# The first head of a two-layer attention trunk: other loading order, two tiles projected together

## The reference, cut to what matters

```python
D_MODEL, SEQ, DEPTH, N_HEADS, HEAD_DIM = 1024, 512, 2, 8, 128
for i in range(DEPTH):                      # layer 0: MoBA attention, layer 1: forgetting attention
    hdn = rms_norm(x, norm_g[i])
    proj = hdn @ w_in[i]                    # 1024 x 4096 (layer 1: 8 columns more)
    q, k, v, z = split(proj, 4)             # 8 heads of 128 columns each
    q = rms_norm(split_heads(q), q_norm)    # layer 0: then rotary, by cos and sin tables
    k = rms_norm(split_heads(k), k_norm)
    y = attention(q, k, v)                  # 512 positions, causal
    y = merge_heads(y) * silu(z)
    x = x + y @ w_out[i]
```

## Time and profile before

| | |
|---|---|
| median of the runs | 595.29 us |
| the profiled execution | 596.05 us |
| its span on the core | 594.3 us |
| PE busy | 579.3 us, 97% of the span |
| DVE, POOL, ACT busy | 343.6, 267.3, 249.1 us |

### The profile page before, as it was taken

One profiled execution on the slowest core, in us unless ns is written; L12 is line 12 of the kernel. 1 busy time (PEld: TensorE's weight loads), 2 busy tenths in 40 slices (PEclk: granted clock), 3 DMA queues, 4 the chain that ended last, 5 costly groups with the idle time before them and its releaser, 6 DMA issues.

```text
span 594.3 us, 9968 instructions
## 1 busy us (share of the span) xinstructions
PE 579.3 (97%) x3219; PEld 538.6 (91%) x3219; DVE 343.6 (58%) x825; ACT 249.1 (42%) x759; POOL 267.3 (45%) x318
## 2 busy tenths in 40 slices
PE   5799999999999999999999999999999999999998
PEld 4689999999999999888899799999999999998887
DVE  4946766767685949464640074747473737373721
ACT  5535353536262635242541254445362626351500
POOL 4664554536372827063662053536362627270600
PEclk9899999999999999999996699999999999999999
DMA  9532322223131313024422024422331335131221
GB/s 284 152 106 81 99 66 77 72 71 88 53 88 53 104 38 124 18 72 137 120 70 75 0 72 71 75 69 60 83 88 53 88 53 90 51 107 34 72 89 53
DMA packets 77195, 48.36 MB, mean 81 GB/s; under 512 B 4080, under 2 KB 71408, under 8 KB 77168
## 3 DMA queue, kind: packets, MB, share of 16 engines
q1 hardware_dynamic: 77168, 48.02, 30.1%
HBM read 45.91 MB, written 2.10 MB: 81 GB/s over the span
## 4 chain that ended last, share of the span: by engine, by line
PE 88%; DVE 4%; DMA 3%; SPq 2%; ACT 1%; issue 1%; POOL 1%
PE banks L295 24%; PE banks L297 24%; PE banks L296 24%; PE banks L402 5%; PE banks L387 3%; PE banks L354 2%; DMA w_raw<-in_b_w_in_dram 2%; PE banks L372 2%; PE banks L376 2%; PE banks L371 2%; DMA first_raw<-in_a_w_in_dram 1%; SPq L230 1%; DVE probs L677 1%; PE banks L375 1%; DVE hT_lo L685 1%
## 5 line engine op out<-in xcount | busy, mean ns | idle before, releaser
L959 POOL TENSOR_TENSOR w_lo<-w_raw,w_hi 128x512 fp32r<-128x512 f32 x152 | 193.6, 1302 | 69.3 <-ACT w_hi L524 69.3
L295 PE MATMUL banks<-w_hi,hT_hi 128*128 128x384 f32 x512 | 176.5, 345 | 6.9 <-DVE qkn L740 5.3
L296 PE MATMUL banks<-w_lo,hT_hi 128*128 128x384 f32 x512 | 172.3, 337 | 0.0
L297 PE MATMUL banks<-w_hi,hT_lo 128*128 128x384 f32 x512 | 172.3, 336 | 0.0
L974 POOL TENSOR_TENSOR msq<-ssq,eps 128x2 f32<-128x2 f32 x64 | 13.9, 217 | 206.6 <-ACT junk L551 206.6
L295 PEld LDWEIGHTS banks<-w_hi,hT_hi 128*128 128x128 f32 x512 | 97.2, 190 | 8.1 <-DVE qkn L740 6.0
L524 ACT ACTIVATE w_hi<-w_raw 128x512 fp32r<-128x512 f32 x152 | 87.4, 646 | 24.1 <-DMA w_raw<-in_b_w_in_dram 14.4
L296 PEld LDWEIGHTS banks<-w_lo,hT_hi 128*128 128x128 f32 x512 | 97.0, 190 | 0.0
L297 PEld LDWEIGHTS banks<-w_hi,hT_lo 128*128 128x128 f32 x512 | 96.8, 189 | 0.0
L551 ACT ACTIVATE junk<-banks 128x128 bf16<-128x128 f32 x128 | 34.3, 274 | 121.4 <-PE banks L297 121.4
L818 DVE RECIPROCAL gz<-gz 128x128 f32<-128x128 f32 x64 | 58.1, 930 | 0.5
(11 more groups left out here) (107 smaller groups left out, 931.7 us busy)
## 6 DMA issues: line engine op xcount, KB each, us to landing
w_raw<-in_b_w_in_dram SPq DMA_DIRECT2D x64, 256.0 KB, 3.7
w_raw<-in_a_w_in_dram SPq DMA_DIRECT2D x56, 256.0 KB, 3.0
w_raw<-in_w_out_dram SPq DMA_DIRECT2D x32, 256.0 KB, 2.9
xs<-in_x_dram SPq DMA_DIRECT2D x4, 512.0 KB, 6.6
first_raw<-in_a_w_in_dram SPq DMA_DIRECT2D x8, 256.0 KB, 5.8
out_dram<-xs SPq DMA_DIRECT2D x7, 256.0 KB, 2.1
gz<-in_norm_g_dram SPq DMA_DIRECT2D x2, 512.0 KB, 4.4
cos_t<-in_rope_cos_dram SPq DMA_DIRECT2D x1, 256.0 KB, 5.5
```

Of the source, the lines that this page charges most:

```text
L295: pe.matmul(dst, ah, bh, start=first and m == 0, stop=False)
L296: pe.matmul(dst, ah, bl, start=False, stop=False)
L297: mm = pe.matmul(dst, al, bh, start=False, stop=last and m == n - 1)
L959: pool.tensor_tensor(w_lo[:, slot, k, :], raw, f32(w_hi[:, slot, k, :]), ALU.subtract).then_inc(wlo_set, by)
```

## The change

It touches only the first head of layer 0; everything from `turn_qk` of head 0 on is issued as before.

- SP: x0 and x1 are loaded ahead of w0 to w7, then x2, tables, x3, and the weights of head 1, whose last four chunks go into `first_raw` (`load_second`). The 512 KB transfer that spread the norm weight goes; ACT issues one row of 4 KB instead.
- PE: two matmuls of 512 columns against a row of ones spread the norm weight into PSUM banks 2 and 5 (`spread_gain`); 2 warm-up transposes instead of 19; tiles 0 and 1 are turned first and projected together, chunk by chunk; each tile of head 0 has its own bank (0, 1, 2, 5), so `qkv` waits for no `qkn_set` there. `zproj` of head 0 writes bank 2 and waits for `qkn_set` 3.
- DVE: both first tiles are normalised before the splits; `norm_x` reads the norm weight from PSUM; chunks 3, 5, 7 of the weights are split on DVE, for head 1 too.
- POOL: chunks 0, 1, 2, 4, 6; the sin tables (four operations) as well as the cos tables, after the factor of tile 3.

```diff
-WARM_UPS = 19
+WARM_UPS = 2
+POOL_FIRST = {0: 1, 1: 1, 2: 2, 4: 2, 6: 2}
+DVE_FIRST = (3, 5, 7)
...
+        def qkv_bank(layer, h, t):
+            return (0, 1, 2, 5)[t] if layer == 0 and isinstance(h, int) and h == 0 else t % 2
...
+            def load_second():
+                for k in range(RAW):
+                    load_chunk(w_raw[:, k, :], head_src(0, 1)(k), raw_in[k])
+                sp.wait_ge(wlo_set, 4)
+                sp.wait_ge(wlo_odd, 1)
+                for k in range(RAW, KC):
+                    load_chunk(first_raw[:, k - RAW, :], head_src(0, 1)(k), first_in[k - RAW])
...
             load_x(0)
-            sp.dma_start(gz[:, :, :].rearrange("p a n -> p (a n)"),
-                         norm_g[0].partition_broadcast(P)).then_inc(gain_in[0], 16)
-            load_first(range(0, 4))
             load_x(1)
-            load_first(range(4, 6))
+            load_first(range(KC))
             load_x(2)
-            load_first(range(6, KC))
             load_tables()
             load_x(3)
+            load_second()
             load_forget()
-            load_job(0, 1, head_src(0, 1))
+            sp.wait_ge(wlo_odd, 2 * len(DVE_FIRST))
...
+            def spread_gain():
+                pe.wait_ge(gain_in[0], 16)
+                for half in range(2):
+                    mm = pe.matmul(banks[:, GAIN_BANKS[half], :], f32(pick[0:1, 0, :]), gz[0:1, half, :],
+                                   start=True, stop=True)
+                mm.then_inc(gain_spread, 1)
...
                 wait(pe, gate_set, g)
+                if isinstance(g, int) and g == 0:
+                    pe.wait_ge(qkn_set, 3)
...
+                    spread_gain()
                     warm_up()
                     turn_hidden(layer, 0)
-                    for t in range(TILES):
-                        qkv(layer, 0, 0, t, (lambda: turn_hidden(layer, t + 1)) if t + 1 < TILES else None)
+                    turn_hidden(layer, 1)
...
+                    for k in range(2, KC):
+                        first_w(0, k)
+                        qkv_part(layer, 0, 0, 0, (k,))
+                        qkv_part(layer, 0, 0, 1, (k,))
+                        if k == 6:
+                            turn_hidden(layer, 2)
+                    pe.wait_ge(xn_set, 2 * TILES)
+                    qkv_part(layer, 0, 0, 2, range(4))
+                    turn_hidden(layer, 3)
+                    qkv_part(layer, 0, 0, 2, range(4, KC))
+                    qkv_part(layer, 0, 0, 3, range(KC))
...
# ACT, first(0):
                     square_x(layer, 0)
-                    split_w(layer, 0, 0, (0, 1))
+                    square_x(layer, 1)
+                    split_w(layer, 0, 0, (0,))
                     split_hidden(layer, 0)
...
+                    split_w(layer, 0, 0, (2, 3, 4, 5))
                     square_x(layer, 2)
+                    split_w(layer, 0, 0, (6, 7))
+                    square_x(layer, 3)
+                    split_hidden(layer, 2)
+                    read_qkv(layer, 0, 0, 0)
+                    read_qkv(layer, 0, 0, 1)
+                    split_w(layer, 1, 1, (0, 1))
+                    split_hidden(layer, 3)
...
# DVE, first(0):
                     norm_x(layer, 0)
-                    split_w_odd((1,))
+                    norm_x(layer, 1)
                     split_hidden(layer, 0)
...
+                    split_first_w(0, (3, 5))
                     norm_x(layer, 2)
+                    split_first_w(0, (7,))
+                    scale_gain()
+                    norm_x(layer, 3)
                     split_hidden(layer, 2)
...
```

More of the change, by code:

```diff
@@ L317, in turn_hidden, with qkv_part @@
                     mm.then_inc(hT_turned, 1)
[L319 to L328, removed]
+            def qkv_part(layer, h, slot, t, ks):
+                for k in ks:
@@ L335, in qkv @@
                                  (w_hi[:, slot, k, 0:3 * P], w_lo[:, slot, k, 0:3 * P]))], k == 0, k == KC - 1)
-                mm.then_inc(a_done, 1)
+                if k == KC - 1:
+                    mm.then_inc(a_done, 1)
+            def qkv(layer, h, slot, t):
+                a = TILES * (HEADS * layer + h) + t
+                wait(pe, qkn_set, a - 1)
+                if isinstance(a, int) and a == TILES:
+                    for k in range(KC):
+                        first_w(1, k)
+                        qkv_part(layer, h, slot, t, (k,))
+                    return
+                if t == 0:
+                    pe.wait_ge(wlo_set, KC * (JOBS * layer + h + 1))
+                qkv_part(layer, h, slot, t, range(KC))
@@ L338, in zproj, with first_w @@
+            def first_w(j, k):
+                if k in DVE_FIRST:
+                    pe.wait_ge(wlo_odd, len(DVE_FIRST) * j + DVE_FIRST.index(k) + 1)
+                else:
+                    pe.wait_ge(wlo_set, KC * j + sum(by for n, by in POOL_FIRST.items() if n <= k))
             def zproj(layer, h, slot):
@@ L670, in norm_x @@
                 buf = normed(layer, t)
+                if layer == 0:
+                    dve.wait_ge(gain_spread, 1)
+                    gain = [banks[:, b, :] for b in GAIN_BANKS]
+                else:
+                    dve.wait_ge(gain_in[layer], 16)
+                    gain = [gz[:, half, :] for half in range(2)]
                 dve.wait_ge(xrs_set, n + 1)
-                dve.wait_ge(gain_in[layer], 16)
                 wait(dve, hT_turned, 2 * (n - 1) if layer or t == 3 else 0)
@@ L722, in norm_qk @@
                     for m in range(2):
-                        last = dve.scalar_tensor_tensor(out=qkn[:, t, m, :], in0=banks[:, t % 2, m * P:(m + 1) * P],
+                        last = dve.scalar_tensor_tensor(out=qkn[:, t, m, :], in0=banks[:, qkv_bank(layer, h, t), m * P:(m + 1) * P],
                                                         scalar=rstd[:, t % 2, m:m + 1], in1=cos_t[:, 0, m, :],
@@ L999, in first @@
                     rstd_x(layer, 0)
[L1000 removed]
                     rstd_x(layer, 1)
[L1002 to L1003 removed]
+                    for k, by in POOL_FIRST.items():
+                        if k == 6:
+                            rstd_x(layer, 2)
+                        split_w(layer, 0, 0, (k,), by=by)
+                    rstd_x(layer, 3)
                     pool.wait_ge(tables_set, 1)
+                    half = P // 2
                     for m in range(2):
+                        for a in range(2):
+                            pool.tensor_tensor(sin_t[:, :, m, a * half:(a + 1) * half],
+                                               sin_t[:, :, 1, a * half:(a + 1) * half],
+                                               bcast(gains[:, m, (1 - a) * half:(2 - a) * half], TILES), ALU.mult)
                         folded = pool.tensor_tensor(cos_t[:, :, m, :], cos_t[:, :, 1, :],
```

136 lines of the change are left out of this document (68 added, 68 removed).

## The result

The changed kernel took 588.87 us (median of 4 runs, 587.64 to 588.92), the kernel before, beside it on the same chip, 595.19 (595.04 to 595.59). The ratio is 0.9883, 95% interval 0.9871 to 0.9895: faster by 6.3 us, where 8.8 were forecast. The time lies inside the range of 584.6 to 590.4, but outside the likeliest case's own range of 585.4 to 587.6, by 1.3 us.

What follows compares the result with a forecast made beforehand. PE bounds the kernel, with 15.0 us idle, nearly all in the first head. `turn_qk` moving from 46.66 to 37.9 saves 8.8 us: 595.29 - 8.8 = 586.5 us, range 584.6 to 590.4.

Steps and rivals of the forecast that it cites:

- the likeliest case: Head 0: z begins between 31.3 and 33.5 us, total 585.4 to 587.6 us; chance 0.55.
- Each microsecond earlier there is one off the total: PE reaching `turn_qk` of head 0 earlier shortens the total equally; 46.66 to 37.9 us gives 8.8 us.
- signs of being wrong: New profile: clock 0.5 beyond 16 us, tile 2 after 23, new PE waits after `turn_qk`, sin above 1.2, x3 after 19.
- signs of being right: `turn_qk` near 37.9, 0.8 us `qkn` wait before z, none before tiles, sin 0.8 near 19.8, normalisation at 7.3, halves 0.74.
- Rival 4: PE in head 0: without 17 warm-ups the clock never rises, `turn_qk` at 57.5, 606.1 us; chance 0.03 with other losses.
- The spread and the normalisations: PE and DVE, head 0: norm weight spread by two matmuls, ready at 7.3 us; each normalisation half takes 0.74 us.
- The pair: PE projects tiles 0 and 1 together from 11.7 us, until 20.9, or 22.3 with the first three microseconds at low clock.
- 14.1 + 1.18/0.324 = 17.7: Load queue: x3 lands at 17.7 us instead of 19.3, counting its bytes at 324 GB/s.
- rival 3: PE, tiles 2 and 3: the low clock returns, 48 matmuls add 7.5 us; 591 to 594 us, chance 0.05.
- The tables on POOL: POOL, from 19.8 us: four sin operations 3.2 us (1.6 to 5.9), two cos 2.95; tables ready at 25.95.
- The wait for `qkn` 3 is the last one: PE ahead of head 0's z: `qkn` 3 at 32.3 us, wait ends at 32.4, 0.8 us after PE is free.
- rival 1: POOL's table chain is longer or x3 no earlier (19.3), shifting everything behind: 587.6 to 590.8 us; chance 0.25.

Runs made afterwards that it cites:

- experiment 4: The kernel before, with only an own bank for each tile of head 0 (no tile waits for `qkn`, z waits for `qkn` 3): 589.46 us, ratio 0.9887.
- after: The changed kernel, with the whole change, against the kernel before: 588.87 us, ratio 0.9883; its profiled execution took 588.92 us.
- experiment 5: The changed kernel, with the norm weight spread by the 512 KB transfer and read from SBUF, no spread matmuls: 591.58 us, ratio 0.9941.
- experiment 1: The changed kernel, with SP issuing head 1's weights only once x3 has landed: 587.67 us, ratio 0.987.
- experiment 2: The changed kernel, with x3 loaded ahead of the tables and the q norm weight scaled after tile 3's normalisation: 586.79 us, ratio 0.9849.
- experiment 6: The changed kernel without the pair: tile 0 whole, then tile 1 with tile 2's transposes in its middle: 587.91 us, ratio 0.988.
- experiment 3: The changed kernel, with 22 transposes that nobody reads put on PE ahead of tile 2: 590.71 us, ratio 0.989.
- experiment 7: The changed kernel, with layer 1's 8-column matmuls put between wide ones of tiles 1 to 3, tile 0's at the end: 582.69 us, ratio 0.9784.
- before: The kernel without the change, timed beside the changed one: 595.19 us; its profiled execution took 596.05 us.
- experiment 8: The changed kernel, with x3 ahead of the tables, layer 1's narrow matmuls between wide ones and weight chunk 1 rounded earlier: 579.81 us, ratio 0.9743.

## Why the prediction was right, and where it was not

**Right in sign, cause and range, not in size.** "Each microsecond earlier there is one off the total" holds in nine kernels to 0.5 us, once layer 1's stretch is counted by itself. That the waits for shared banks were the loss is shown by experiment 4. The head gave 5.5 us of the 8.8 that the forecast has for it. What layer 1 gave, of which the forecast knew nothing, brought the time nearer to it by luck; without it the time would be about 595.3 - 5.5 = 589.8 us, still inside the range, near its upper end.

Of the forecast's own signs of being wrong three came: x3 landed after 19 (19.86), tile 2 began after 23 (24.15), and the granted clock was 0.50 beyond 16 us (24.8 to 28). Of its signs of being right these came: no wait for `qkn` before a tile, PE's wait ahead of z put down to DVE's `qkn`, sin at 0.7 us, the first normalisation at 7.00, and no new wait behind `turn_qk`. Rival 4 did not come: with 17 warm-ups fewer the pair still ran at 1.00 from 12.37, behind spread matmuls and transposes that had PE busy from 3.18 to 11.3 but for 0.22 us.

**The spread and the normalisations.** Forecast 7.3 and 0.74 a half; measured 7.00 and the rows below (line 747 of after by duration, ns min/median/max, first and last start): 742 to 748 ns in layer 0, where the weight is in PSUM, and up to 1775 in layer 1, where it is in SBUF.

```profile
L747 DVE SCALAR_TENSOR_TENSOR probs<-xs,ssx,banks x4: 742/742/748, 8.3 to 22.7; 128x512 f32<-128x512 f32 x4
...
L747 DVE SCALAR_TENSOR_TENSOR probs<-xs,ssx,gz x4: 751/926/1775, 278.4 to 291.9; 128x512 f32<-128x512 f32 x4
...
L747 DVE SCALAR_TENSOR_TENSOR xn<-xs,ssx,banks x2: 742/744/747, 16.9 to 17.6; 128x512 f32<-128x512 f32 x2
```

Tile 2's, from 16.94, run beside this split of POOL's:

```profile
16.81 1.29 POOL L1022 TENSOR_TENSOR w_lo<-first_raw,w_hi 128x512 fp32r<-128x512 f32 x1
```

With the weight in SBUF the same place took 2.37 us for the two instead of 1.41 (experiment 5). The Trainium skill (SBUF — State Buffer, "SBUF: two separate sides") has it that a DVE operation with two SBUF inputs and a GpSimd operation that reads SBUF shut each other out for a whole instruction; both rows agree, and the forecast's term was right.

**The pair.** 12.37 for 11.7, and done at 21.8 (24.15 less the gap of 2.34), inside 20.9 to 22.3.

**The step that failed: x3.** The term was "14.1 + 1.18/0.324 = 17.7"; it landed at 19.86. The sum took the queue to serve loads in the order of issue, and a load to be whole when its bytes had been counted at the stream's mean rate. Until 19.86 the queue moved 284 GB/s, 5.64 MB, of which x, head 0's weights and the tables are 4.85: 0.79 MB of head 1's weights, issued later, were served before x3 was whole. Holding them back gives 0.8 us (experiment 1). The other 1.37 of the 2.16 us are the thin end of the stream in experiment 1, where the last 0.15 MB took 2.07 us at 73 GB/s. The dip at the tables, 0.5 us of bytes, had been made up by then. With x3 ahead of the tables at most 0.7 us of lateness is left (experiment 2). From x3's landing on, the forecast's chain was right: 4.25 us to tile 2 by its times, 4.29 measured.

**What followed from it.** Tile 2 came 1.95 us late, which made a gap of 2.34 us, and the low clock behind it cost 1.6. This is rival 3, at a fifth of its price: it had 7.5 us for 48 matmuls, and twelve and some transposes were slow. Less 0.4 for the smaller wait ahead of z and plus 0.1 in z, that is 3.3: 41.16 for 37.9. The gap was also made by the pair's being early (experiment 6). That the gap brings the low clock is borne out by the other profiles. Experiments 1, 2, 3 and 6, with no gap there, keep 1.00 through 24 to 28 us. Experiments 5 and 7, with gaps of 2.10 and 2.44 us, took 3.63 and 3.54 us for the twelve matmuls behind them, as after did, and experiment 4, with 1.54 us, took 2.22. A run that fills a true gap is missing.

**The tables on POOL.** The term was 6.2 us and measured 5.2: sin 1.41 us for two, 0.7 each for 0.8 (well inside 0.41 to 1.48), cos 1.27 to 1.28 for 1.48. "The wait for `qkn` 3 is the last one" held: it is the 0.41 us ahead of z. But it was not the tables that set it. The factor was there at 28.07 and used at 30.35, since DVE's program has the half split of tile 3 ahead of `norm_qk`, and that one waits for PE. The forecast's working lacked this order on DVE. By its own times the omission cost nothing: tile 3 turned at 24.3 and 2.47 us from there to `norm_qk`, as in experiment 2, make 26.8 (an estimate), against 26.9 for the factor. The late tile 2 made it count. So the number fell into rival 1's band, of which one half held (x3 late) and the other not (tables longer).

**The term that was missing.** 1.7 us of the profiled gain are from layer 1's low stretch. The forecast asked only where PE was idle, and there it never is. The page's row of granted clock (tenths, in 40 slices of the span) had it all along. Before:

```profile
PEclk9899999999999999999996699999999999999999
```

## What to carry to other kernels

When a wait goes, look at the next one's releaser to the end. Do not take a load to be whole when its bytes are counted: loads behind it took 0.8 us, and with none behind it the last 0.15 MB still took 2.07 us. Issue the critical load ahead of those that can wait, here the tables. Take each part of a change by itself: the banks alone gave a time that can't be told from that of the whole. Work that ends early only to wait may cost more than its wait, if the clock falls in the gap. And read the clock row also where PE is 100% busy: the largest gain here, 6 us, lay in matmuls that the change never touched.

## What was not expected of the hardware

- Matmuls of 8 columns with a whole weight load each came 0.11 us apart at first, PE busy 1.00 in every window, and the granted clock fell to 0.50 during them and stayed there for 17.1 or 20.5 us, into the wide matmuls behind. Mixed with wide ones (experiments 7 and 8) it stayed at 1.00 until the last separate group, then 6.8 or 3.4 us at 0.50. What decides between 17.1 and 20.5 is open: before and experiments 3 and 4 had the longer one, each in one profile, so it may as well vary between executions of one kernel as between kernels. It makes 1.7 us, more than a quarter of what this change is worth, and the times of one kernel can stand further apart than that: experiment 7's four were 581.2 twice and 584.2 twice.
- Behind the same instructions on PE, the pair's first matmul took 0.66 us, at the low clock, in experiments 1 to 3 and 0.41 in after, and the transposes of tile 2 came 1.6 to 2.0 us later. In these profiles the low clock was paid either there or behind the gap that an early pair leaves. What decides which is open.
- Loads issued later on a queue take part of the rate before an earlier one is whole (0.8 us on a 512 KB load). With nothing behind it, that load's end came at 73 GB/s for 2.07 us, the DMA share at 0.19 (experiment 1). While the tables were in flight the stream fell to 192 to 263 GB/s, where it ran at 320 to 373 just before; with x3 ahead of them it fell later, to 254 (experiment 2).
